# Triangular inverse of a gated-delta layer: 64x64 tile products replaced by packed whole-chunk products

## What is computed

```python
lower = jnp.einsum('bhnid,bhnjd->bhnij', k_beta, k) * decay * strict
a_mat = lower + jnp.eye(C, dtype=f32)
rhs = jnp.concatenate([v_beta, k_beta * jnp.exp(g)[..., None]], axis=-1)
sol = lax.linalg.triangular_solve(a_mat, rhs, left_side=True, lower=True, unit_diagonal=True)
...
def step(S, inp):
    q_c, qk_c, u_c, w_c, g_c, gl_c, kt_c = inp
    v_new = u_c - jnp.einsum('bhck,bhkv->bhcv', w_c, S)
    o = (jnp.einsum('bhck,bhkv->bhcv', q_c * jnp.exp(g_c)[..., None], S)
         + jnp.einsum('bhij,bhjv->bhiv', qk_c, v_new))
    S = S * jnp.exp(gl_c)[..., None, None] + jnp.einsum('bhck,bhcv->bhkv', kt_c, v_new)
    return S, o
```

## Time and profile before

| | |
|---|---|
| median of 3 runs | 1925.32 us |
| lowest and highest | 1924.72 and 1926.5 us |
| span of the profiled execution | 1924.2 us |
| TensorE busy in the profiled execution | 1879.1 us, 98% |
| VectorE, ScalarE, GpSimd busy | 1555.3, 859.7, 776.2 us |

### The profile page before, as it was taken

How to read it: one execution, slowest core, us unless ns; L and a number is a source line. 1 busy time by engine, 2 the same in 40 slices (tenths; PEclk the granted TensorE clock), 3 DMA queues, 4 the chain that set the end, 5 groups by cost and what they waited for, 6 DMA issues and landing times.

```text
span 1924.2 us, 33735 instructions
## 1 busy us (share of the span) xinstructions
PE 1879.1 (98%) x12681; PEld 1697.5 (88%) x12681; DVE 1555.3 (81%) x3015; ACT 859.7 (45%) x1507; POOL 776.2 (40%) x579
## 2 busy tenths in 40 slices
PE   6999999999999999999999999999999999999998
PEld 3779999999977899999999888888888888888887
DVE  4567777777666788997886698889889989898998
ACT  3524444444434234478888443433333333343433
POOL 0000000000024433697876155555545655555662
PEclk9999999999999999999999999999999999999999
DMA  9722222221272424767777999999999999999984
GB/s 394 280 103 72 83 72 72 73 72 56 83 287 74 142 71 144 229 195 222 214 216 201 315 375 384 381 390 383 388 377 373 395 383 379 376 372 372 371 340 155
DMA packets 179728, 474.72 MB, mean 247 GB/s; under 512 B 16752, under 2 KB 79184, under 8 KB 176240
## 3 DMA queue, kind: packets, MB, share of 16 engines
q1 hardware_dynamic: 133488, 304.78, 45.0%
q0 software_dynamic: 46080, 167.79, 22.9%
HBM read 426.57 MB, written 45.94 MB: 246 GB/s over the span
## 4 chain that ended last, share of the span: by engine, by line
PE 53%; DVE 10%; DMA 2%; issue 1%; POOL 1%; ACT 0%; DVEq 0%; ACTq 0%
PE dd L2767 17%; PE pp L2754 16%; PE pp L2767 8%; PE pp L2374 7%; PE dd L2722 4%; DMA x<-in_v,idx 1%; POOL hot_a L2534 1%; DVE top_i L2417 1%; DVE top_i L2406 1%; DVE top L3012 1%; DVE less L2407 1%; DVE top_v L2401 1%; DVE top_v L2412 1%; PE pp L465 1%; DVE cand L3124 1%
## 5 line engine op out<-in xcount | busy, mean ns | idle before, releaser
L449 ACT ACTIVATE w_hi<-w_raw 128x1024 fp32r<-128x1024 f32 x202 | 212.9, 1054 | 164.9 <-PE pp L465 107.9
L465 PE MATMUL pp<-act_hi,w_hi 128*128 128x272 f32 x1040 | 236.2, 308 | 2.2 <-ACT qt L2820 1.2
L453 DVE TENSOR_TENSOR w_lo<-w_raw,w_hi 128x1024 fp32r<-128x1024 f32 x173 | 212.5, 1229 | 30.7 <-ACT w_hi L449 30.6
L465 PE MATMUL pp<-act_hi,w_lo 128*128 128x272 f32 x1040 | 214.7, 288 | 0.0
L465 PE MATMUL pp<-act_lo,w_hi 128*128 128x272 f32 x1040 | 214.7, 288 | 0.0
L2949 ACT ACTIVATE co_hi<-cf 128x384 fp32r<-128x384 f32 x126 | 66.3, 526 | 320.0 <-PE pp L2767 256.9
L2754 PE MATMUL pp<-act_hi,w_hi 128*128 128x384 f32 x616 | 208.8, 339 | 0.0
L2754 PE MATMUL pp<-act_lo,w_hi 128*128 128x384 f32 x616 | 207.6, 337 | 0.0
L2754 PE MATMUL pp<-act_hi,w_lo 128*128 128x384 f32 x616 | 207.1, 336 | 0.0
L2534 POOL TENSOR_SCALAR hot_a<-cst,gcols 128x128 f32<-128x128 f32 x144 | 191.0, 1334 | 39.7 <-PE dd L2722 39.3
L465 PEld LDWEIGHTS pp<-act_hi,w_hi 128*128 128x128 f32 x1040 | 161.2, 189 | 18.5 <-issue 10.5
(11 more groups left out here) (485 smaller groups left out, 4636.6 us busy)
## 6 DMA issues: line engine op xcount, KB each, us to landing
w_raw<-in_stream SPq DMA_DIRECT2D x206, 512.0 KB, 4.7
v_raw<-in_v SPq DMA_DIRECT2D x128, 512.0 KB, 6.6
ada_w<-in_ada SPq DMA_DIRECT2D x24, 1024.0 KB, 10.5
gt<-gate_matrix SPq DMA_DIRECT2D x31, 768.0 KB, 8.5
gate_matrix<-gstage SPq DMA_DIRECT2D x11, 2048.0 KB, 10.2
early<-cst SPq DMA_DIRECT2D x50, 192.0 KB, 4.2
cst<-early SPq DMA_DIRECT2D x50, 192.0 KB, 8.7
wrow<-in_wout SPq DMA_DIRECT2D x8, 512.0 KB, 8.1
```

The source lines that it names most:

```text
L449: nc.scalar.activation(w_hi[k.slot][:], w_raw[k.slot][:], ACT.Copy).then_inc(w_hi_done, 1)
L453: nc.vector.tensor_tensor(w_lo[k.slot][:], w_raw[k.slot][:], w_hi[k.slot][:].bitcast(F32), ALU.subtract).then_inc(w_lo_done, 1)
L465: last = nc.tensor.matmul(pp[s][:, b, 0:HN], w[:, c * P:(c + 1) * P], a[:, c, b * HN:(b + 1) * HN], start=(c == 0 and w is w_hi[s] and a i ...
```

## The change

All 13 products of a head become the same helper, `level_product`. For each of the four chunks it does one matmul with the whole 128x128 chunk of the left operand as weights and, as moving operand, only those 64 columns of the right operand's chunk which that level needs (`merged` picks one half of every pair of blocks, so at level 0 it is runs of two columns, at level 5 one run of 64). The result is written packed: 64 columns for each chunk, 256 (`HALF`) in the bank. No matmul of the inverse addresses a quarter of the array any more. On the readers' side the PSUM operands of L1745, L1750, L1758, L1763 and L1508 become packed views of the same number of elements, and up to level 3 `ap_[n]` is stored packed too. Level 5's copy on ScalarE takes 64 partitions in place of 128.

With this go: the memset of PSUM bank 1 on VectorE at the start of the block (L1537) with TensorE's wait for it (`bank_zero`), four of the six memsets of `ap_` on GpSimd (L1153), and in every head VectorE's memset of `tu` at level 5 (L1761).

```diff
-        def diagonal_blocks(bank, left, right):
+        def level_product(bank, n, left, right):
 
             for c in range(NC):
-                for b in range(2):
-                    rows, t = slice(B2 * b, B2 * (b + 1)), slice(c * P + B2 * b, c * P + B2 * (b + 1))
-                    last = nc.tensor.matmul(dd[rows, bank, t], left[rows, t], right[rows, t], start=True, stop=True)
+                t = slice(c * P, (c + 1) * P)
+                last = nc.tensor.matmul(packed(dd[:, bank, c * B2:(c + 1) * B2], n), left[:, t], right(c), start=True, stop=True)
             return last
...
-        def cells(t, n):
-            return t.rearrange("p (c b two s) -> p c b two s", c=NC, two=2, s=2 << n)[:, :, :, 0, :]
+        def cells(n):
+            if n <= LAST_32:
+                return by_chunk(ap_[n][:, 0:HALF], n)
+            return ap_[n][:].rearrange("p (c b two s) -> p c b two s", c=NC, two=2, s=2 << n)[:, :, :, 0, :]
...
-                        if n < NLV - 1:
-                            last = diagonal_blocks(1, lt, ti)
-                        else:
-                            for c in range(NC):
-                                lo, hi = upper_halves(c)
-                                last = nc.tensor.matmul(dd[HI, 1, lo], lt[LO, hi], ti[LO, lo],
-                                                        start=True, stop=True)
-                        last.then_inc(a_done, 1)
+                        level_product(1, n, lt, lambda c: merged(ti[:, c * P:(c + 1) * P], n, 0)).then_inc(a_done, 1)
                         beside(f"level {n}")
                         pe.wait_ge(tu_ready, (NLV + 1) * hv + n + 1)
                         gate_pe(pe, ap_ready, NLV * hv + n + 1)
                         if n < NLV - 1:
-                            diagonal_blocks(2, tu, ap_[n]).then_inc(dti_done, 1)
-                        if n == LAST_32 + 1:
+                            level_product(2, n, tu, lambda c: correction(n, c)).then_inc(dti_done, 1)
+                        if n > LAST_32:
                             gate_pe(pe, qkm_ready, hv + 1)
-                            diagonal_blocks(3, ap_[n], tu).then_inc(dtu_done, 1)
...
+                            level_product(3, n, ap_[n],
+                                          lambda c: merged(tu[:, c * P:(c + 1) * P], n, 1)).then_inc(dtu_done, 1)
...
-                nc.vector.memset(dd[:, 1, :], 0.0).then_inc(bank_zero, 1)
...
-                            nc.vector.tensor_tensor(part(ti[:], n, 0), part(ti[:], n, 0), part(dd[:, 2, :], n, 0),
+                            nc.vector.tensor_tensor(part(ti[:], n, 0), part(ti[:], n, 0), packed(dd[:, 2, 0:HALF], n),
                                                     ALU.subtract).then_inc(ti_ready, 1)
...
-                            nc.vector.memset(tiles(tu[HI, :])[:, :, 0:B2], 0.0)
                             dve.wait_ge(dtu_done, 2 * hv + 2)
```

More of the change, by code:

```diff
@@ L1056, in build, with merged, packed @@
         B2 = P // 2
-        def diagonal_blocks(bank, left, right):
+        HALF = NC * B2
+        def merged(t, n, half):
+            return t.rearrange("p (b two s) -> p b two s", two=2, s=2 << n)[:, :, half, :]
+        def packed(t, n):
+            return t.rearrange("p (b s) -> p b s", s=2 << n)
+        def level_product(bank, n, left, right):
             for c in range(NC):
-                for b in range(2):
-                    rows, t = slice(B2 * b, B2 * (b + 1)), slice(c * P + B2 * b, c * P + B2 * (b + 1))
-                    last = nc.tensor.matmul(dd[rows, bank, t], left[rows, t], right[rows, t], start=True, stop=True)
-            return last
-        def upper_halves(c):
-            return slice(c * P, c * P + B2), slice(c * P + B2, (c + 1) * P)
+                t = slice(c * P, (c + 1) * P)
+                last = nc.tensor.matmul(packed(dd[:, bank, c * B2:(c + 1) * B2], n), left[:, t], right(c), start=True, stop=True)
+            return last
         LO, HI = slice(0, B2), slice(B2, P)
@@ L1076, in part, with by_chunk, correction @@
             return t.rearrange("p (b two s) -> p b two s", two=2, s=2 << n)[:, :, half, :]
-        def cells(t, n):
-            return t.rearrange("p (c b two s) -> p c b two s", c=NC, two=2, s=2 << n)[:, :, :, 0, :]
+        def by_chunk(t, n):
+            return t.rearrange("p (c b s) -> p c b s", c=NC, s=2 << n)
+        def cells(n):
+            if n <= LAST_32:
+                return by_chunk(ap_[n][:, 0:HALF], n)
+            return ap_[n][:].rearrange("p (c b two s) -> p c b two s", c=NC, two=2, s=2 << n)[:, :, :, 0, :]
+        def correction(n, c):
+            if n <= LAST_32:
+                return packed(ap_[n][:, c * B2:(c + 1) * B2], n)
+            return merged(ap_[n][:, c * P:(c + 1) * P], n, 0)
         def masked(n):
@@ L1151, in _ @@
                 retire(pool, ended)
-                for n in range(NLV):
+                for n in range(LAST_32 + 1, NLV):
                     nc.gpsimd.memset(ap_[n][:], 0.0).then_inc(ap_zero, 1)
@@ L1250, in head @@
                     if not has_prior(hv):
-                        pe.wait_ge(bank_zero, 1)
                         pe.wait_ge(ones_rounded, 1)
@@ L1507, in head @@
                             act.wait_ge(a_done, NLV * hv + NLV)
-                            nc.scalar.activation(part(ap_[n][:], n, 0), part(dd[:, 1, :], n, 0),
+                            nc.scalar.activation(part(ap_[n][HI, :], n, 0), packed(dd[HI, 1, 0:HALF], n),
                                                  ACT.Copy).then_inc(ap_ready, 1)
@@ L1740, in head @@
                     if not has_prior(hv):
-                        dve.wait_ge(ap_zero, NLV)
+                        dve.wait_ge(ap_zero, NLV - 1 - LAST_32)
                     for n in range(NLV):
```

10 lines of the change are left out of this document (5 added, 5 removed).

## The result

The changed kernel takes **1939.87 us** (median of 4 runs, 1939.52 to 1941.03) against 1925.91 (1924.72 to 1926.83) for the kernel before on the same chip: ratio 1.0074, 95% interval 1.006 to 1.0088, 14.0 us slower. The spans of the two profiled executions are 1938.2 and 1924.2. The forecast was 1938.6, in a range of 1934.8 to 1942.3.

What follows compares the result with a forecast made beforehand. TensorE's queue was taken to bound the heads' block. 1.68 us a head, 13.4 for eight, -0.40 at the start and +0.3 for first and last heads gave 13.3: span 1937.5, median 1938.6, range 1934.8 to 1942.3.

Steps and rivals of the forecast that it cites:

- The pace of a pass: New whole-chunk products: the weight load sets 0.111 us a pass, 0.89 a product, 1.78 for level 4's pair.
- What a product costs now: Kernel before, between projection pairs: 0.81 or 0.82 us a lone product, 1.27 for level 4's pair, including holes.
- The side sum: The skill's 107 ns per weight load over the block's 832 passes: 3.3 us less, 1935.5; not used.
- Strided reads: Rival: short runs of moving columns at levels 0 and 1 read at quarter speed, +26 us, 1965; chance 3%.
- Level 0's two products: Level 0 of each head: the ti correction already waits and cannot load weights ahead; together +0.26 us.
- The new waits: A products of levels 1, 2 and 4: VectorE's later hand-over makes each wait 0.09 us.
- the wait for `tu`: End of level 5: the 0.08 us wait for `tu` goes with VectorE's memset.
- Once, at the start: Start of the heads' block: without VectorE's bank memset TensorE's 0.45 us wait goes, -0.40 us.
- The four memsets on GpSimd: Removed GpSimd memsets run beside everything: 0 us.
- the rest of the +0.3: First and last head: no wait for `tu` before in the first, less cover in the last; together +0.3 us.
- both rivals in which the moving columns matter: New passes: moving columns set the pace, 0.06 us, 1893, chance 3%; or about 0.095 us, 1925, chance 5%.
- No new waits: Rival: VectorE hands over quicker than added up, -2.2 us, 1936.4; within the forecast's range.

Runs made afterwards that it cites:

- e1: The changed kernel with all 128 moving columns streamed per product in place of 64, six GpSimd memsets again: 1943.26 us, ratio 1.0087 to the kernel before.
- e3: The changed kernel with level 5's two products loading only the 64 weight columns needed, still on 128 rows: 1940.53 us (one run).
- e2: The changed kernel with VectorE's two waits ahead of the subtraction from ti exchanged: 1938.82 us, ratio 1.0066 to the kernel before.
- e4: The kernel before with 32x32 tiles for a products and ti corrections of levels 0 to 3, ScalarE clearing bank 2 each head: 1913.23 us, ratio 0.9931.

## Why the prediction was right

**The pace of a pass** (0.111 us, "the weight load sets the pace") held: 0.90 for a lone product against the 0.89 taken, 1.78 for level 4's pair as taken, and e1 shows it apart from the moving columns. The argument of the earlier trace rows, that 32 moving columns are no faster than 128, carried over to 64. The readers, put at nothing, took 0.42 us as before.

**What a product costs now** was right in its sums and wrong in its parts. The prediction called the holes 0.10 on entry and one as large on the way back. The way back was never read: from the first pair behind a product to the second it is 0.35 before and 0.34 in the whole-array form. The visit costs 0.35 in all (e3). The forecast did not suffer, as it used distances between pairs that hold the whole price. The side sum with 0.107 in place of 0.111 should read 1938.6 - 3.3 = 1935.3, not 1935.5; the forecast does not use it.

**Strided reads cost nothing.** Level 0's a product reads runs of two columns and waits for nothing:

```profile
181.21 1.00 PE L1072 MATMUL dd<-ti,lt 128*128 128x64 f32 x8
...
182.35 0.41 PE L465 MATMUL pp<-act_lo,w_hi 128*128 128x272 f32 x2
```

The second pair behind it starts 182.35 - 180.96 = 1.39 after the pair ahead, as at level 1's correction (1.40), which has longer runs, and in e1, which has none (1.39).

**Level 0's two products** were put at +0.26 and measured +0.25: 4.80 against 184.12 - 179.57 = 4.55 before, where the pair ahead is this row of the kernel before:

```profile
179.57 0.41 PE L465 MATMUL pp<-act_hi,w_lo 128*128 128x272 f32 x2
```

**The new waits** at the a products of levels 1, 2 and 4 exist, and e2 shows that they are on the path. They cost 1.51 - 1.40 = 0.11 at level 1 and 0.10 at levels 2 and 4, not 0.09: the reader's start was put at 1.12 behind the slot and came at 1.11. Only 0.03 to 0.04 of this is a later start; the other 0.07 is lost behind it, as a product that is held up loads its weights late: 0.03 ahead of itself in place of 0.12, as in level 0's rows above, and the next pair comes 0.89 behind its start in place of 0.81.

**Mis-sized terms.** The head was put at +1.68 and came at +1.81 on the average of heads two to seven. The pieces that I can name: three waits at 0.10 or 0.11 for 0.09 (0.04); the product's own difference, 0.09 for 0.08, in nine lone products beside those of level 0 (up to 0.09); and the wait for `tu`, which was to vanish and left 0.04 (0.42 against 0.38 undisturbed). That is 0.17 where 0.13 was missing; distances that are read to 0.01 and taken nine times allow no better.

**Once, at the start**, -0.40 was put down for the memset, and the first product came 0.24 earlier. That is 117.41 to 117.38, with the changed run standing 0.2 later before the block (GpSimd's first memset starts at 115.78, and at 115.58 before). The brackets on VectorE's instructions say why: ahead of the memset VectorE had waited 0.29, and without the memset it waits 0.42 ahead of L1623. So the memset had hidden 0.13 of this wait. The step that failed is the -0.40: it took the memset's whole length for gain and did not ask what is late next when the memset goes.

**The four memsets on GpSimd** were put at 0, "beside everything". That term is wrong too. The first head was put at 1.68 + 0.08 and grew by 1.42 only, as a wait of TensorE went. Before, and in the changed kernel:

```profile
119.38 0.97 PEld L1263 LDWEIGHTS dd<-kb,qkv_h 128*128 128x128 f32 x8 [0.32 <-DVE kb L1720]
```

```profile
118.98 0.98 PEld L1278 LDWEIGHTS dd<-kb,qkv_h 128*128 128x128 f32 x8
```

From the last pair ahead of this product to the second pair behind it it takes 2.20 before and 1.83 after, 0.37 less. The list of the earlier trace rows does not show the wait, since it ends on the weight load and not on the matmul. In all five kernels here with two memsets the distance is 1.83, and in the four with six it is 2.19 to 3.06. The last section shows VectorE's part in it.

**The end of the block.** The last head took 2.28, where 1.68 and the rest of the +0.3, some 0.2, had been put down. In it the first use of `tu` waits more than elsewhere (0.48 for its two passes, 0.38 before), as the three passes ahead of it are shorter than a piece of the projection (0.70 against 0.75). Another 0.16 lies at the very end. Before, and in the changed kernel:

```profile
551.49 1.23 DVE L453 TENSOR_TENSOR w_lo<-w_raw,w_hi 128x1024 fp32r<-128x1024 f32 x1 [0.44 <-ACT w_hi L449]
...
553.04 1.13 PE L1950 MATMUL dd<-cst,hs 128*128 128x128 f32 x8 [0.93 <-PEq L1148]
```

```profile
564.95 1.06 ACT L449 ACTIVATE w_hi<-w_raw 128x1024 fp32r<-128x1024 f32 x1 [1.39 <-DMA w_raw<-in_stream]
...
566.04 1.22 DVE L453 TENSOR_TENSOR w_lo<-w_raw,w_hi 128x1024 fp32r<-128x1024 f32 x1 [0.60 <-ACT w_hi L449]
...
567.59 1.13 PE L1951 MATMUL dd<-cst,hs 128*128 128x128 f32 x8 [1.09 <-PEq L1164]
```

The next block begins when all engines have ended this one. TensorE is through first and waits 0.93 us before and 1.09 after; the last of the compute engines to end is VectorE with its weight split, which waits for ScalarE's half and that for a DMA. In all nine kernels TensorE's next product starts 0.32 to 0.33 behind the end of L453, with TensorE idle for 0.93 to 1.64 us. So the sentence that what is added to TensorE's queue is added to the end holds up to its last product in the block and not for the end itself. In e4 the last head's own products were 1.6 us shorter, and the wait took 0.7 of it back. What decides when this DMA lands was not tested, and some 0.1 us of the last head has no name.

**The sum.** With its start (14.58 - 0.24) the block cost 14.3 in place of 13.3. The span grew by 14.0, as the first product of the heads stood 0.03 earlier and the rest behind the block was 0.5 shorter, which is within its spread. That 1938.6 came within 1.3 us of 1939.87 is in part luck: heads two to seven (0.8), the last (0.4) and the start (0.2) were put too low, the first head was put 0.3 too high, and the rest of the program happened to be 0.5 shorter.

**The rivals.** e1 rules out both rivals in which the moving columns matter. The level-0 row above rules out the strided reads. *No new waits* falls with e2.

## What to carry to other kernels

When short products stand between long matmul streams, price them by the weight columns of each step (0.111 us at 128, 0.058 at 64, 0.032 at 32), plus about 0.35 us for each visit if they leave part of the array out; the moving side was free up to 128 columns under 128 weight columns. Two products behind one another pay for one visit only. So 64 columns in place of 128 gain little in a lone product of eight steps (0.09) and much in a pair (0.51). Small independent blocks paid here in small tiles even with four times as many instructions: here 32 passes of 32x32 take 0.58, the visit included, where eight of 128x64 take 0.90. A product that gets longer also hands over later, so look up at the same time how much cover the reader and the next product have, and order the reader's queue so that the result just finished comes before work that nobody waits for. And look at both ends of a block, where another engine than the busy one can be the last.

## What the runs showed of the hardware

- **A float32 pass at 128 weight columns takes 0.111 us** with 32, 64 or 128 moving columns; 64 moving columns were the same contiguous or in runs of two. With 64 weight and 64 moving columns it is 0.058, on 64 or 128 rows (before, e3), and a step of four passes of 32x32 is 0.032 (e4). The rule in the Trainium skill, "TensorE: Matmul & The Clock Gate", section "LDWEIGHTS (loading the stationary operand)", columns over 1.2 GHz, gives an estimated 107 ns for the load of 128 columns. Every form with 128 weight columns and no more than 128 moving ones showed 0.111, and the measurement decides.
- **Leaving the whole-array form and coming back costs about 0.35 us a visit**: 0.35 for 64x64, 0.34 for 128 rows with 64 columns (e3), 0.33 for 32x32 (e4), whatever the number of steps between. 0.09 of it stands ahead of the product (0.34 to 0.35 from a pair to it, where the whole-array form has 0.25). The Trainium skill, "TensorEngine Tiling (Array Packing)", section "Key Properties", says that a change of tiling mode drains the engine and gives no price; the runs fit that and add the price.
- **A held-up product loses 0.08 us beyond its wait**: its weights load 0.03 ahead of it in place of 0.12, and the next pair starts 0.89 behind it in place of 0.81 (changed kernel, levels 0, 1, 2 and 4).
- **The order of two waits ahead of a VectorE instruction is worth 0.07 us** (e2: it starts 1.04 behind the product when the late wait is listed first, 1.11 when it is listed second).
- **VectorE work was stretched beside GpSimd's memsets.** The copy `hs` takes 0.18 in the changed kernel, where the two memsets have ended, and 1.50 in e1, where six run on beside it; it ends within 0.04 of them. In e4 it takes 1.26:

```profile
116.18 2.83 POOL L1164 MEMSET ap<- 128x512 f32 x6 [40.48 <-POOLq L520]
...
117.79 1.26 DVE L1585 COPY hs<-tok 128x30 f32<-128x30 f32 x1
...
119.08 0.88 DVE L1590 TENSOR_SCALAR decay<-decay,hs 128x128 f32<-128x128 f32 x4
```

  In the kernel before, with the same six memsets, the copy takes 0.34 and it is the group behind it that is stretched:

```profile
117.18 0.34 DVE L1570 COPY hs<-tok 128x30 f32<-128x30 f32 x1
117.56 1.18 DVE L1575 TENSOR_SCALAR decay<-decay,hs 128x128 f32<-128x128 f32 x4
```

  The Trainium skill, "GPSIMD Engine Reference", section "8. Key points", says that the two engines share their interfaces to SBUF and that VectorE instructions in a two-port mode, or with two SBUF inputs, contend with GpSimd. The rows fit that: with two memsets, over before the copy starts, five kernels have 0.18 for the copy and 0.87 for the group; with six, four kernels have one or the other stretched. But no run here took the memsets away alone, so the cause is argued and not shown, and why it is now the one instruction and now the other stays open.
